# A software-pipelined chunk loop with u tiles inside it, in the gMLP mixer of a two-layer trunk

## What is computed

```python
def _chunk_gmlp_mixer(a, w_in, ln_g, ln_b, w_s, b_s, w_out):
    n, L, _ = a.shape
    c = min(L, CHUNK)                       # CHUNK = 128
    z = jax.nn.gelu(a @ w_in)
    u, v = jnp.split(z, 2, axis=-1)
    v = _layernorm(v, ln_g, ln_b)
    mask = jnp.tril(jnp.ones((c, c), dtype=bool))
    w = jnp.where(mask[None], w_s[:, :c, :c], 0).astype(v.dtype)
    vg = v.reshape(n, L // c, c, H_A, DH_A)
    s = jnp.einsum('hts,nkshd->nkthd', w, vg) + b_s[:, :c].T...
    y = u * s.reshape(n, L, E_A)
    return y @ w_out, v
```

## Time and profile before

| what | us |
|---|---|
| three timed runs, median | 6395.32 |
| their lowest and highest | 6331.39 and 6410.49 |
| the profiled execution | 5812.11 |
| its span, slowest core (core 0) | 5811.0 |
| spans of the eight cores in it | 5802.5 to 5811.0 |

### The profile page before, as it was taken

The page is one execution under the profiler, slowest core; times in us unless marked ns, Lnnn a source line. Parts: engine busy times, 40 slices in busy tenths (PEclk is TensorE's granted clock), DMA queues, the critical chain, the costliest instruction groups (busy, mean ns, idle before and its releaser), DMA issues.

```text
span 5811.0 us, 78422 instructions; the slowest of 8 cores (5802.5 to 5811.0 us)
## 1 busy us (share of the span) xinstructions
PE 5312.2 (91%) x33576; PEld 3368.2 (58%) x33576; DVE 1203.0 (21%) x2551; ACT 538.4 (9%) x1286; POOL 812.7 (14%) x724
## 2 busy tenths in 40 slices
PE   5999999977598999999779999997999899999976
PEld 3555555544365666666446666664665566666644
DVE  3011010132413010111340111113332201011135
ACT  2000000021002000000220000001000200000020
POOL 0111111100011111111011111111111111111110
PEclk7999999978698999999789999998999899999978
DMA  4777777644275878787367787874787588877734
GB/s 90 67 65 68 66 65 67 62 44 44 20 72 49 73 74 76 72 74 72 39 55 70 73 76 71 76 72 48 73 76 68 48 74 74 75 73 73 70 40 93
DMA packets 1405550, 382.98 MB, mean 66 GB/s; under 512 B 1398884, under 2 KB 1402628, under 8 KB 1402824
## 3 DMA queue, kind: packets, MB, share of 16 engines
q0 software_dynamic: 1395968, 354.46, 67.1%
q1 hardware_dynamic: 9240, 23.50, 1.2%
HBM read 723.53 MB, written 8.93 MB: 126 GB/s over the span
## 4 chain that ended last, share of the span: by engine, by line
PE 89%; DVE 5%; ACT 3%; issue 2%; DMA 2%; ACTq 0%; DVEq 0%; SPq 0%
PE pa_u L319 45%; PE pb_u L319 40%; PE pst_u L342 2%; ACT sq_u L339 2%; DVE xn_u L352 1%; DMA x_tok_u<-xin 1%; ACT sig_u L428 1%; DVE buf_u L555 1%; DMA p_tok_u<-pin 0%; DVE st_u L519 0%; DVE fst_u L780 0%; DVE yo_u L794 0%; DVE rstd_u L349 0%; PE x_pt_u L259 0%; DVE vhb_u L532 0%
## 5 line engine op out<-in xcount | busy, mean ns | idle before, releaser
L319 PE MATMUL pa_u<-xn_u,wsl_u 128*128 128x348 bf16 (+3 forms) x11904 | 1870.4, 315 | 95.0 <-DVE xn_u L352 69.3
L319 PE MATMUL pb_u<-xn_u,wsl_u 128*128 128x348 bf16 (+3 forms) x10368 | 1621.0, 314 | 0.0
L319 PEld LDWEIGHTS pa_u<-xn_u,wsl_u 128*128 128x128 bf16 x11904 | 1160.0, 98 | 771.5 <-issue 112.9
L319 PEld LDWEIGHTS pb_u<-xn_u,wsl_u 128*128 128x128 bf16 x10368 | 1007.6, 97 | 578.6
L319 PE MATMUL pa_u<-buf_u,wsl_u 128*128 128x348 bf16 (+3 forms) x4992 | 787.6, 316 | 29.4 <-DVE buf_u L400 23.0
L319 PE MATMUL pb_u<-buf_u,wsl_u 128*128 128x348 bf16 (+3 forms) x4992 | 779.1, 314 | 0.0
L400 DVE TENSOR_TENSOR buf_u<-pb_u,sg_u 128x348 bf16<-128x348 f32 (+1 forms) x528 | 247.2, 524 | 2356.6 <-PE pb_u L319 2356.6
L319 PEld LDWEIGHTS pa_u<-buf_u,wsl_u 128*128 128x128 bf16 x4992 | 487.3, 98 | 314.0 <-issue 37.7
L319 PEld LDWEIGHTS pb_u<-buf_u,wsl_u 128*128 128x128 bf16 x4992 | 485.1, 97 | 276.0
L391 ACT ACTIVATE sg_u<-pa_u 128x348 f32<-128x348 f32 (+1 forms) x528 | 209.4, 470 | 3221.6 <-PE pa_u L319 3221.6
L303 POOL DMA_DIRECT2D wsl_u<-ffn_w_gate x176 | 201.4, 1144 | 1344.2 <-PE pa_u L319 1343.3
(11 more groups left out here) (108 smaller groups left out, 1007.1 us busy)
## 6 DMA issues: line engine op xcount, KB each, us to landing
wsl_u<-ffn_w_gate POOLq DMA_DIRECT2D x176, 512.0 KB, 7.9
wsl_u<-ffn_w_up POOLq DMA_DIRECT2D x176, 512.0 KB, 8.0
wsl_u<-ffn_w_down POOLq DMA_DIRECT2D x128, 480.0 KB, 7.5
wsl_u<-ffn_w_down POOLq DMA_DIRECT2D x64, 448.0 KB, 6.7
wsl_u<-c_w_in POOLq DMA_DIRECT2D x48, 512.0 KB, 7.5
wsl_u<-a_w_in POOLq DMA_DIRECT2D x32, 512.0 KB, 7.9
wsl_u<-ple_w_gate POOLq DMA_DIRECT2D x32, 512.0 KB, 7.6
x_tok_u<-xin SPq DMA_DIRECT2D x9, 1024.0 KB, 7.1
```

What stands on the lines that cost most here:

```text
L319: last = nc.tensor.matmul(pset[ti][:, 0:tn], lhsT=ws[:, k, :], rhs=rhs_fn(k, t0, tn), start=(k == 0), stop=(k == nk - 1))
```

## The change

All eight PSUM banks are named once at the start and tracked by bank: three for PA, three for PB, and two spare ones, S0 and S1, which serve for transposes and norm sums everywhere.

In the mixer, the chunk loop becomes two functions. `front(j)` holds the transposes (now into S0 and S1), the statistics, the root, the reciprocal, a new small product of minus the mean and the reciprocal, and the normalisation, which is now four ScalarE instructions. `back(j)` holds the mixing matmuls, in four groups of four over the banks A2, B0, B1 and B2, and the scale-and-bias on VectorE. The program emits `front(0)`, the sample part's arithmetic, and then for each j `front(j + 1)`, `back(j)` and two u tiles. A u tile is 16 matmuls into one bank, A0 or A1, and its gelu. Eighteen tiles, which are six of the 16 u columns, are emitted in the loop. The other ten columns follow as groups of 48 matmuls. The products with `buf2` start behind the loop, two columns at a time until they have caught up. `ug` is now bf16, with six buffers.

The sample part's 64 small VectorE operations become six over all feature blocks. Its transposes and output transfers move into the u columns 8 to 11. The three barriers between chunk loop, sample part and u projection go. The writes of the scale-and-bias are tracked under a name of their own (`b2s`), so that the next chunk's transposes don't wait for them.

```diff
--- before.py
+++ after.py
+NU = 6
+PER = 2
...
+        banks = [E(pmt("bank%d" % i, [128, 512], F32)) for i in range(8)]
+        PA, PB, SP0, SP1 = banks[0:3], banks[3:6], banks[6], banks[7]
+        PA_R, PB_R = ["A0", "A1", "A2"], ["B0", "B1", "B2"]
...
-                    pst = ns.enter_context(pmt("pst", [128, 512], F32))
+                    pst = SP0
...
+                    vhb = [G(sbt("vhb%d" % i, [128, D], BF16)) for i in range(2)]
...
+                    ug = [G(sbt("ug%d" % i, [128, 1042], BF16)) for i in range(NU)]
...
-                    with contextlib.ExitStack() as s2:
...
-                        S.barrier()
-                    with contextlib.ExitStack() as s3:
...
-                        S.barrier()
-                    with contextlib.ExitStack() as s4:
...
+                    pv, pr = [SP0[:].bitcast(BF16), SP1[:].bitcast(BF16)], ["S0", "S1"]
+                    MB, MR = [PA[2], PB[0], PB[1], PB[2]], ["A2", "B0", "B1", "B2"]
+
+                    def front(j):
+                        c0 = j * 128
+                        jj = j % 2
+
+                        def emit_tr():
+                            last = None
+                            for c in range(NCH):
+                                last = nc.tensor.transpose(out=pv[c // 8][:, (c % 8) * 128:(c % 8 + 1) * 128],
+                                                           in_=buf2[:, c, c0:c0 + 128], identity=ident_b[:])
+                            return last
+                        S.op("pe", [("b2", c) for c in range(NCH)], [pr], emit_tr)
+
+                        def emit_stats():
+                            last = None
+                            for q in range(4):
+                                last = nc.vector.bn_stats(out=st6[jj][:, q, :], in_=pv[q // 2][:, (q % 2) * 512:(q % 2 + 1) * 512])
+                            return last
+                        S.op("dve", [pr], [("st6", jj)], emit_stats)
+                        S.op("dve", [("st6", jj)], [("mv", jj)], lambda: nc.vector.bn_aggr(
+                            out=mv[jj][:], in_=st6[jj][:].rearrange("p a b -> p (a b)")))
+                        S.op("act", [("mv", jj)], [("rt1", jj)], lambda: nc.scalar.activation(
+                            out=rt1[jj][:], in_=mv[jj][:, 1:2], func=AF.Sqrt, bias=EPS, scale=1.0))
+                        S.op("dve", [("rt1", jj)], [("rs1", jj)], lambda: nc.vector.reciprocal(out=rs1[jj][:], in_=rt1[jj][:]))
+                        S.op("dve", [("rs1", jj), ("mv", jj)], [("nmr", jj)], lambda: nc.vector.scalar_tensor_tensor(
+                            out=nmr[jj][:], in0=mv[jj][:, 0:1], scalar=-1.0, in1=rs1[jj][:], op0=ALU.mult, op1=ALU.mult))
+                        vb = vhb[jj]
+
+                        def emit_vh():
+                            last = None
+                            for q in range(4):
+                                last = nc.scalar.activation(out=vb[:, q * 512:(q + 1) * 512],
+                                                            in_=pv[q // 2][:, (q % 2) * 512:(q % 2 + 1) * 512],
+                                                            func=AF.Identity, bias=nmr[jj][:, 0:1], scale=rs1[jj][:, 0:1])
+                            return last
+                        S.op("act", [pr, ("nmr", jj), ("rs1", jj)], [("vhb", jj)], emit_vh)
+
+                    def back(j):
+                        c0 = j * 128
+                        jj = j % 2
+                        vb = vhb[jj]
+                        for q in range(4):
+                            def emit_mix(q=q):
                                 last = None
+                                for i in range(4):
+                                    c = q * 4 + i
+                                    last = nc.tensor.matmul(MB[q][:, i * 128:(i + 1) * 128],
+                                                            lhsT=vb[:, c * 128:(c + 1) * 128], rhs=wmT[:, c // 2, :],
+                                                            start=True, stop=True)
                                 return last
+                            S.op("pe", [("vhb", jj)] + [("wmT", hh) for hh in range(8)], [MR[q]], emit_mix)
+
+                            def emit_sev(q=q):
                                 last = None
+                                for i in range(4):
+                                    c = q * 4 + i
+                                    last = nc.vector.scalar_tensor_tensor(
+                                        out=buf2[:, c, c0:c0 + 128], in0=MB[q][:, i * 128:(i + 1) * 128],
+                                        scalar=gcol(G_LNG, c), in1=bias2[:, c, :], op0=ALU.mult, op1=ALU.add)
                                 return last
+                            S.op("dve", [MR[q]] + [("bias2", q * 4 + i) for i in range(4)],
+                                 [("b2s", q * 4 + i) for i in range(4)], emit_sev)
+
+                    def sample_path():
...
+                        VF = ["vnf_all"]
+                        b3 = lambda ap: ap.unsqueeze(1).broadcast_to([128, 16, 16])
+                        g3 = lambda g: colt[:, g * 16:(g + 1) * 16].unsqueeze(2).broadcast_to([128, 16, 16])
+                        h4 = lambda t: t[:].unsqueeze(3).broadcast_to([128, 8, 2, 16])
+                        v4d = vnf[:].rearrange("p (h r) n -> p h r n", r=2)
+                        tmp4 = vsf[:, :, 0:16].rearrange("p (h r) n -> p h r n", r=2)
+                        out4 = buf2[:, :, C_SAMP:C_SAMP + 16].rearrange("p (h r) n -> p h r n", r=2)
+                        TTT = nc.vector.tensor_tensor
+                        S.op("dve", [("vsf", c) for c in range(NCH)] + ["ms_"], VF, lambda: TTT(
+                            out=vnf[:], in0=vsf[:, :, 0:16], in1=b3(ms_[:]), op=ALU.subtract))
+                        S.op("dve", VF + ["rss"], VF, lambda: TTT(out=vnf[:], in0=vnf[:], in1=b3(rss[:]), op=ALU.mult))
+                        S.op("dve", VF, VF, lambda: TTT(out=vnf[:], in0=vnf[:], in1=g3(G_LNG), op=ALU.mult))
+                        S.op("dve", VF, VF, lambda: TTT(out=vnf[:], in0=vnf[:], in1=g3(G_LNB), op=ALU.add))
+                        S.op("dve", VF, [("vsf", c) for c in range(NCH)], lambda: TTT(out=tmp4, in0=v4d, in1=h4(w00b), op=ALU.mult))
+                        S.op("dve", [("vsf", c) for c in range(NCH)], [("b2s", c) for c in range(NCH)], lambda: TTT(
+                            out=out4, in0=tmp4, in1=h4(b0b), op=ALU.add))
+
+                    def sample_out(k):
+                        half, q = k // 2, k % 2
+                        pso, sr = v4([SP0, SP1][k % 2]), "S%d" % (k % 2)
+                        vo, vr = vhb[half][:].bitcast(F32), ("vhb", half)
+
+                        def emit_vt():
+                            last = None
+                            for cc in range(4):
+                                last = nc.tensor.transpose(out=pso[0:16, cc, :], in_=vnf[:, k * 4 + cc, :], identity=ident_f[:])
+                            return last
+                        S.op("pe", ["vnf_all"], [sr], emit_vt)
+                        S.op("act", [sr], [vr], lambda: nc.scalar.activation(
+                            out=vo[0:16, q * 512:(q + 1) * 512], in_=pso[0:16, :, :].rearrange("p a b -> p (a b)"),
+                            func=AF.Copy))
+                        if q == 1:
+                            S.dma("sp", [vr], [], ("o", "vs"), lambda: nc.sync.dma_start(
+                                out=vs_out[:, half * 1024:(half + 1) * 1024], in_=vo[0:16, :]))
+
+                    ust = {"ws": None, "n": 0}
+
+                    def u_tile():
+                        c, ti = ust["n"] // 3, ust["n"] % 3
+                        if ti == 0:
+                            ust["ws"] = wget("a_in", 0, 0, 16, c * 128)
+                        ws, wres = ust["ws"]
+                        bank, br = PA[ust["n"] % 2], "A%d" % (ust["n"] % 2)
+                        t0, tn = TT[ti]
+                        ub = ug[c % NU]
+
+                        def emit():
+                            last = None
+                            for k in range(16):
+                                last = nc.tensor.matmul(bank[:, 0:tn], lhsT=ws[:, k, :], rhs=xn[:, k, t0:t0 + tn],
+                                                        start=(k == 0), stop=(k == 15))
+                            return last
+                        S.op("pe", [wres] + XN_ALL, [br], emit)
+                        S.op("act", [br], [("ug", c % NU)], lambda: nc.scalar.activation(
+                            out=ub[:, t0 - 126:t0 - 126 + tn], in_=bank[:, 0:tn], func=AF.Gelu_apprx_tanh))
+                        ust["n"] += 1
+
+                    def y_col(c):
+                        ub = ug[c % NU]
+
+                        def emit_y():
+                            last = None
+                            for ti, (t0, tn) in enumerate(TT):
+                                last = nc.vector.tensor_tensor(out=buf2[:, c, t0:t0 + tn], in0=ub[:, t0 - 126:t0 - 126 + tn],
```

(53 more changed lines are left out.)

191 lines of the change are left out of this document (48 added, 143 removed).

## The result

| what | us |
|---|---|
| timed runs, median (lowest to highest) | 6230.98 (5705.21 to 6633.79) |
| the kernel before beside it | 6316.04 (5810.21 to 6558.09) |
| the profiled execution, and its span (core 6) | 5707.97 and 5706.9 |
| stage from the first transposes to the output matmuls, before and after | 275.06 and 168.35 |

The ratio of the times is 0.9795, with an interval of 0.9729 to 0.9862; a repetition gave 0.9817, interval 0.9793 to 0.9841. Many timed runs of either kernel lie hundreds of us above the profile because the cores of one die or both show a lower granted clock (in the run of 6230.98 cores 0 to 3 have spans of at most 5705.6 and cores 4 to 7 of at least 6210), and the ratios leave these out.

A forecast was written before the change was run, and what follows sets the result against it. The mixer stretch was taken as bound by engines waiting for one another in a serial chain. Terms 16.4 + 69.3 + 10.4 + 71.4 + 2.4 + 3.3 = 173.2 against 275.1 us saved 101.9: 6293 us, range 6230 to 6360.

The forecast's parts named there:

- I take off the same 101.9 there: On the timed runs' median of 6395.3 us, subtract the stage's predicted saving of 101.9 us, giving 6293 us.
- lead-in to chunk 1's product: Mixer, from chunk 0's first transposes to the end of chunk 1's small product, sample arithmetic included: 16.4 us.
- seven turns: Mixer loop, from chunk 1's to chunk 8's small product, mainly VectorE's queue and a table load: 9.9 us each, 69.3 together.
- loop's end: From chunk 8's small product: last mixing 4.8, two u tiles 4.8, gelu freeing their banks 0.8; 10.4 us.
- ten columns and sample output: Behind the loop: the remaining u columns, 10 x 7.14 = 71.4 us, and four groups of sample output transposes, 2.4 us.
- end, gelu and product: Gelu and y product of the last u column, before the output matmuls: 3.3 us.
- the spells eat TensorE's slack first: In the loop, half-clock spells use TensorE's idle time first; slow transposes leak out, 0.8 us in about half the turns.
- hidden at either end: In the loop, ScalarE's normalisation, 2.28 us, lies under the previous chunk's scale-and-bias and does not lengthen the turn.
- A: Rival: TensorE stays at half clock in the loop, turns of 13.3 us, 73 us saved, 6322 us; chance 0.16.
- B: Rival: each ScalarE table switch costs more than its load, 1.28 us ahead of every root; 6302 us; chance 0.09.
- C: Rival: waits around banks A0 and A1 make the loop serial, turns of 27.5 us, 6421 us, slower; chance 0.04.
- D: Rival: root and table load are hidden in the loop, turns of 8.2 us, 12 us more saved, 6281 us; chance 0.09.

The follow-up runs named there:

- the three-tile kernel: Three u tiles a turn instead of two, eight ug buffers, `bias2` in bf16, against the changed kernel: stage 194.6 us, turn 15.1 us, span 5721.7 us.

## Why the prediction was right about the stage and wrong about the time

**The step that failed** is the last one of the sum: "I take off the same 101.9 there". The saving was put on the median of the three timed runs, which made 6293 and 1.6%. The level at which the two kernels are compared is that of the profiled execution, where I had allowed "timed runs at the level of the profiled execution" a chance of 0.1. Runs of the kernel before at that level measured 5810.2 to 5815.4 (the one of 5854.9 apart), so 5812.1 was no lucky run but the kernel's own time; the changed one's are 5700.8 to 5709.8. All eight spans stood between 5802.5 and 5811.0 in the profile of before, and the work in it was accounted for; the 583 us above it, which no view explained, were the part to doubt. With the sum as it stood the time would have been 5710, against 5707.97, and the share 101.9/5812 = 1.75%, so that "within 2%" would have been a near thing and not 0.84. That the median of all timed runs, 6230.98, lies just inside the range of 6230 to 6360 is luck: these runs spread from 5705 to 6634.

**The terms of the stage,** each against the trace of after:

| term | predicted | measured |
|---|---|---|
| lead-in to chunk 1's product | 16.4 | 16.06 |
| seven turns | 69.3 (9.9 each) | 66.05 (9.44 each) |
| loop's end | 10.4 | 10.42 |
| ten columns and sample output | 73.8 | 73.31 |
| end, gelu and product | 3.3 | 2.51 |
| sum | 173.2 | 168.35 |

*The turn.* VectorE's chain was summed as 9.45, and 0.45 was added for transposes at half clock "in about half of the turns". They cost 1.4 us in three of seven turns, 0.2 a turn; one turn in the trace still has them at 1.86. That 9.45 comes so near the mean of 9.44 is partly luck: it was summed for turns with the transposes in time, and the four such turns take 9.26 to 9.28. The clock did fall in spells, as windows of the loop after show:

```profile
1422.00:1432.00 10.00, 7.41 (x63) 5.54 (x61) 7.89 (x25) 6.37 (x9) 1.14 (x1) 0.87 0.58 54
...
1442.00:1452.00 10.00, 7.42 (x71) 5.33 (x70) 7.45 (x24) 6.93 (x10) 0.00 (x0) 1.00 0.30 31
1452.00:1462.00 10.00, 7.41 (x60) 5.86 (x58) 7.25 (x23) 6.30 (x10) 1.14 (x1) 0.83 0.58 55
```

At 0.83 TensorE is busy as long as at 1.00 with fewer matmuls in the window, and VectorE works on nearly as before (7.25 against 7.45). That fits the step that the spells eat TensorE's slack first.

*The lead-in.* The sample operations over 256 columns took 0.36 to 0.43 (0.36 taken). (The sum wrote 16.4 for the lead-in, but its 1412.6 lies only 16.3 behind the start at 1396.28.) The sums ended 6.9 us after the transposes began, 8.1 was allowed; the root of the samples did wait behind the normalisation, and VectorE was free of them 1412.64 - 1400.17 = 12.5 after the start, as in the sum. The last term was 1416.23 - 1412.55 = 3.68 (3.75 taken), from the statistics' start at 1412.55 on:

```profile
1406.46 2.79 ACT L563 ACTIVATE vhb_u<-bank_u,nmr_u,rs_u 128x512 bf16<-128x512 bf16 x4 [0.63 <-DVE nmr_u L556]
1407.15 0.17 DVE L605 TENSOR_SCALAR ms__u<-bank_u 128x16 f32<-128x16 f32 x1 [0.78 <-PE bank_u L601]
...
1409.13 0.22 ACT L611 ACTIVATE rts_u<-var_u 128x16 f32<-128x16 f32 x1
...
1412.21 0.43 DVE L628 TENSOR_TENSOR buf_u<-vsf_u,b0b_u 128x256 bf16<-128x256 f32 x1
1412.55 2.48 DVE L548 BATCH_NORM_STATS2 st_u<-bank_u 128x6 f32<-128x512 bf16 x4
...
1416.07 0.16 DVE L556 SCALAR_TENSOR_TENSOR nmr_u<-mv_u,rs_u 128x1 f32<-128x1 f32 x1
```

*The normalisation on ScalarE* took 2.79 where 2.28 was priced, and "hidden at either end" did not quite hold: the next statistics can start 4.3 after the small product at full clock (3.6 summed), where VectorE would be free after 4.1, and 5.1 in the turn with transposes of 1.86 (4.4 summed). What shows is 0.2 a turn, and more in the slow turns.

*The end.* The product of the last column, priced at its old 1.38 for three, takes 0.84: `ug` is now bf16, an effect that the change part left out.

**The rivals.** A (half clock throughout, 13.3 a turn) did not come; the mean clock was 0.92. B (a switch costs more than its load): the root starts 0.01 to 0.02 behind the end of the load, so no. C (the serial ring) was argued away with a margin of 10.8 against 12 us, and that held for two tiles; the three-tile kernel shows that the ring is real and one tile away. D (8.2, root and load hidden) did not come, since both were on VectorE's chain; with the load taken away the turn is 8.05.

## What to carry to other kernels

When timed runs lie far above a profile in which the spans of all cores agree, and no view explains the gap, put a saving and its share on the level of the profile. In a loop that spans engines with in-order queues, price the turn by the busiest engine's own list, each operation and each wait that its neighbour can't hide; here that gave 9.45, against 9.26 to 9.28 in the turns with nothing late and 9.44 in the mean. Then walk every ring of buffers through the queues (who reads a bank out, what stands ahead of that reader), since one more tile turned a margin of a microsecond into a wait of four.

## What the runs showed of the hardware

**A table switch costs its load and hardly more.** The load at 1428.39 starts 0.01 behind the end of four busy instructions, and the gelu starts 0.02 behind the load's end; there are two switches a turn. With the gelus deferred, the first read-out starts 2.66 behind the start of the normalisation instead of 4.10, so this switch cost 1.44, 0.16 more than its load. The one on the chain cost VectorE 1.68 - 0.40 = 1.28 of waiting; taking it away gave 1.39 a turn, of which late transposes explain 0.14. The Trainium skill (ScalarE: Activation LUTs, What ACT_TABLE_LOAD costs) states 1.28 for the load, which agrees, and a drain of 1.38 besides, which no run here shows. The Trainium skill (same page, same section) gives about 93 ns for each operand that ScalarE takes by pointer; the normalisation has two and the gelu none, and it took 2.79 where the gelu's rate gave 2.28. An estimate from that figure of the Trainium skill is 4 x 2 x 0.093 = 0.74 more; measured are 0.51 more, which agrees in sign. The function is not the reason (a read-out of 348 columns takes 0.47 with Identity and 0.46 with gelu); whether it is the pointers or the bf16 input, no run shows.

**More TensorE work made a turn shorter.** Turns of 10.15 with one tile, 9.44 with two, and clocks of 0.83 and 0.92 beside them; the gain sits in one wait, VectorE's for the transposes (6.6 and 1.4 us in seven turns). With the gelus deferred, where the turn is 8.05 for the same two tiles, the clock was 1.00.
